# A two-layer fp32 transformer stack on one core: free banks for the first products after each boundary, retention's value products among its gates, and stick-breaking split into weights and values

## The reference, cut to what matters

```python
# first block
h = h + rmsnorm(hybrid_mixer(rmsnorm(h)))            # gated delta rule + convolution module
h = h + rmsnorm(memory_cross_attention(rmsnorm(h)))  # 4 heads of 256
h = h + rmsnorm(conv_glu_ffn(rmsnorm(h)))            # up 2*2816, causal conv, silu(a)*b, down
# second block, layer 0: retention, 4 heads, q and k 256 wide, v and gate 512 wide
q = rope(q); k = rope(k) / 16
o_t = sum_{s<=t} gamma_h^(t-s) (q_t . k_s) v_s
o = (o - mean(o)) * rsqrt(var(o) + eps);  y = (o * silu(g)) @ ret_w_out
# second block, layer 1: stick-breaking attention, 8 heads, q and k 128 wide, v 256 wide
A[t,s] = sigmoid(z_ts) * prod_{s<j<t} (1 - sigmoid(z_tj)),   s < t,   z = q k^T / sqrt(128)
y = ((A @ v) * silu(g)) @ sb_w_out
```

## Time and profile before

| | |
|---|---|
| timed runs, median of 3 | 1875.31 us (1871.51, 1875.31, 1875.56) |
| profiled execution | 1869.74 us, of which the span of instructions is 1868.0 us |
| PE busy | 1778.4 us, 95% of the span, 9647 products |
| PEld, DVE, ACT, POOL busy | 1450.4, 1009.3, 674.2, 177.2 us |
| granted TensorE clock, mean | 0.984 |
| HBM traffic | 144.09 MB read, 78 GB/s over the span |

### The profile page before, as it was taken

The page is one execution under the profiler, slowest core; times in us unless marked ns, Lnnn a source line. Parts: engine busy times, 40 slices in busy tenths (PEclk is TensorE's granted clock), DMA queues, the critical chain, the costliest instruction groups (busy, mean ns, idle before and its releaser), DMA issues.

```text
span 1868.0 us, 23478 instructions
## 1 busy us (share of the span) xinstructions
PE 1778.4 (95%) x9647; PEld 1450.4 (78%) x9647; DVE 1009.3 (54%) x1492; ACT 674.2 (36%) x1002; POOL 177.2 (9%) x155
## 2 busy tenths in 40 slices
PE   6899998999999999999999999999999999999987
PEld 5677787789789888888897776877698777787765
DVE  3668788446426954945864633435455333443434
ACT  4443343445335322322351222222154443434342
POOL 0153544210010000000100000000010000000001
PEclk9999899999999999999999999999999999999999
DMA  5111112242112232322322131322122222222211
GB/s 187 35 47 46 35 59 78 79 147 80 42 61 80 91 105 76 113 90 87 135 74 87 58 103 67 107 73 79 59 80 79 66 70 79 69 89 68 90 46 45
DMA packets 44937, 147.70 MB, mean 79 GB/s; under 512 B 4768, under 2 KB 8736, under 8 KB 44832
## 3 DMA queue, kind: packets, MB, share of 16 engines
q1 hardware_dynamic: 44832, 146.21, 23.7%
HBM read 144.09 MB, written 2.10 MB: 78 GB/s over the span
## 4 chain that ended last, share of the span: by engine, by line
PE 85%; DVE 10%; ACT 2%; issue 2%; POOL 1%; DMA 0%; SPq 0%; DVEq 0%; ACTq 0%; POOLq 0%
PE ps L414 29%; PE ps L409 19%; PE ps L410 18%; PE ps L411 18%; DVE sl L1768 1%; DVE acc L1959 1%; DVE ca L1819 1%; PE ps L1000 1%; DVE y L2137 0%; ACT sh L1148 0%; DMA raw<-in_wqkv 0%; DVE pad L1810 0%; POOL dg L2595 0%; DVE ss L1925 0%; DVE ca L1815 0%
## 5 line engine op out<-in xcount | busy, mean ns | idle before, releaser
L1148 ACT ACTIVATE sh<-raw 128x1024 fp32r<-128x1024 f32 x260 | 271.5, 1054 | 570.1 <-PE ps L411 445.3
L1768 DVE TENSOR_TENSOR sl<-raw,sh 128x1024 fp32r<-128x1024 f32 x260 | 322.6, 1251 | 175.9 <-ACT sh L1148 175.8
L409 PE MATMUL ps<-xh,sh 128*128 128x512 f32 x640 | 264.0, 412 | 3.0 <-DVE up L2265 1.5
L411 PE MATMUL ps<-xl,sh 128*128 128x512 f32 x640 | 252.2, 394 | 0.0
L410 PE MATMUL ps<-xh,sl 128*128 128x512 f32 x640 | 251.8, 393 | 0.0
L409 PE MATMUL ps<-sh,xh 128*128 128x512 f32 x384 | 154.7, 403 | 5.6 <-DVE tm L2350 4.0
L411 PE MATMUL ps<-sl,xh 128*128 128x512 f32 x384 | 149.8, 390 | 0.0
L410 PE MATMUL ps<-sh,xl 128*128 128x512 f32 x384 | 149.7, 390 | 0.0
L409 PEld LDWEIGHTS ps<-xh,sh 128*128 128x128 f32 x640 | 121.8, 190 | 32.6 <-issue 2.8
L410 PEld LDWEIGHTS ps<-xh,sl 128*128 128x128 f32 x640 | 121.9, 190 | 26.0 <-issue 2.6
L411 PEld LDWEIGHTS ps<-xl,sh 128*128 128x128 f32 x640 | 121.5, 190 | 26.4
(11 more groups left out here) (353 smaller groups left out, 3256.5 us busy)
## 6 DMA issues: line engine op xcount, KB each, us to landing
raw<-in_wup SPq DMA_DIRECT2D x44, 512.0 KB, 3.5
raw<-in_wdn SPq DMA_DIRECT2D x24, 512.0 KB, 3.4
raw<-in_rqk SPq DMA_DIRECT2D x16, 512.0 KB, 3.5
raw<-in_rv SPq DMA_DIRECT2D x16, 512.0 KB, 3.5
raw<-in_rg SPq DMA_DIRECT2D x16, 512.0 KB, 4.2
raw<-in_rout SPq DMA_DIRECT2D x16, 512.0 KB, 3.5
raw<-in_sv SPq DMA_DIRECT2D x16, 512.0 KB, 3.4
raw<-in_sg SPq DMA_DIRECT2D x16, 512.0 KB, 3.5
```

The source lines that it names most:

```text
L409: e.matmul(dst, wh, ah, start=start, stop=False, skip_group_check=True)
L411: return e.matmul(dst, wh, al, start=False, stop=stop, skip_group_check=True)
L1148: e.activation(SH[j % NSPL][:], RAW[j % NRAW][:], ACT.Copy).then_inc(*hi(j))
L1768: e.tensor_tensor(SL[j % NSPL][:], RAW[j % NRAW][:], SH[j % NSPL][:].bitcast(F32), ALU.subtract).then_inc(*lo(j))
```

## The change

1. **Free banks** (tables `QB`, `up_bank`, `RVB`, `SVB`): the fifth slab behind a boundary goes to a bank that is free already. In the attention and in the FFN's first part it is bank 6 in place of 0; in retention's first head the value slabs use banks 6, 5, 0, 1 in place of 0, 1, 2, 3; in stick-breaking's first pair 6, 0, 1, 2.
2. **Low parts first**: in the FFN's down products DVE makes the low part of the slab ahead before it adds the finished bank to `y`, and not behind. In the gates of retention it makes it before the background steps. At the end of each part of the up products one low part moves ahead of three convolution taps; a wait of DVE on itself now stands there alone.
3. **Retention**: the value products no longer wait for `gated`, so they stand among the gate slabs; the four products with the gates come after `gated`, all four in one step. `sqb` has four buffers in place of two. One empty step less.
4. **Stick-breaking**: `stick` is cut into `weights` and `values`, and the list is weights(p,0), weights(p,1), values(p,0), values(p,1). `values` waits for the gates and for v. For the last pair the gates come before v (in the weight order too), and ACT copies two of the four v banks. Before the absolute value ACT loads the table set that holds both exp and log, in place of one load before each of these two.
5. **The end**: for the last layer POOL adds only tiles 0 to 3, in both halves; PE adds 4 to 7.

```diff
-        o += [("sv", 4 * p + i) for i in range(4)]
-        o += [("sg", 4 * p + i) for i in range(4)]
+        v, g = [("sv", 4 * p + i) for i in range(4)], [("sg", 4 * p + i) for i in range(4)]
+        o += g + v if p == 3 else v + g
...
+        QB = (0, 1, 2, 3, 6, 1, 2, 3)
+        RVB = ((6, 5, 0, 1), (0, 1, 2, 3), (0, 1, 2, 3), (0, 1, 2, 3))
+        SVB = ((6, 0, 1, 2), (0, 1, 2, 3), (0, 1, 2, 3), (0, 1, 2, 3))
+        def up_bank(part, i):
+            return 6 if part == 0 and i == 4 else i % 4
...
@@ PE, retain @@
-                while not gated[h]:
-                    yield
                 for tb in range(NB):
...
                     rel[B] = [(rtv, ("n", h, tb))]
                     yield
-                yield
+                while not gated[h]:
+                    yield
                 yield
...
@@ PE, stick @@
-            def stick(p, h):
+            def weights(p, h):
...
+            def values(p, h):
+                ZZ = ZZS[h]
                 for et in range(2):
-                    while flow["hold"] or (p, 2 * h + et) not in flow["g"]:
+                    while flow["hold"] or (p, 2 * h + et) not in flow["g"] or p not in flow["v"]:
                         yield
...
-                bg.add(stick(p, 0))
-                bg.add(stick(p, 1))
+                for part in (weights, values):
+                    for h in range(2):
+                        bg.add(part(p, h))
...
+                for part in ("gv" if p == 3 else "vg"):
...
@@ ACT, weights @@
+                e.preload_act_table_set("natural_log_exp_and_others")
...
@@ ACT, v of the last pair @@
+                            for tb in (1, 3):
+                                ac.wait_ge(*used[j + 3 if tb == 3 else (j + 3, tb)])
+                                ac.wait_ge(*stm[("o", p - 1, 1, 1)])
+                                e.activation(VS[:, tb, :], PS[SVB[p][tb]][:], ACT.Copy,
+                                             scale=RC[:, tb:tb + 1]).then_inc(*sta(("v", p, tb)))
...
@@ DVE, up @@
+                if i == 2 * FFN[part][1] - 2 * a0 - 2:
+                    low(j + i + 5)
...
@@ DVE, down products @@
                     if m >= 3:
                         beat(2)
+                    low(j + m + 4)
                     if part:
                         y_add(("y3", part, m), m, j + m, m if m < 3 else m % 4,
                               ya[("y3", m)] if part == 1 else yv[("y3", 1, m)])
-                    low(j + m + 4)
...
@@ DVE, retain @@
-                    if tb >= 2:
-                        ve.wait_ge(*rtv[("g", h, tb - 2)])
-                    e.tensor_scalar(SQB[tb % 2][:], b[:], BN[:, tb, 6:7], BN[:, tb, 8:9], ALU.subtract,
+                    if h:
+                        ve.wait_ge(*rtv[("g", h - 1, tb)])
+                    e.tensor_scalar(SQB[tb][:], b[:], BN[:, tb, 6:7], BN[:, tb, 8:9], ALU.subtract,
                                     ALU.mult).then_inc(*rtv(("n", h, tb)))
+                while not gated[h]:
+                    yield
+                for tb in range(NB):
                     ve.wait_ge(*rta[("g", h, tb)])
                     ve.wait_ge(*rtv[("n", h, tb)])
-                    e.tensor_tensor(GR[:, tb, :], GR[:, tb, :], SQB[tb % 2][:], ALU.mult).then_inc(*rtv(("g", h, tb)))
-                yield
+                    e.tensor_tensor(GR[:, tb, :], GR[:, tb, :], SQB[tb][:], ALU.mult).then_inc(*rtv(("g", h, tb)))
                 yield
...
@@ DVE, gates of retention @@
                 for g in range(4):
+                    low(j + 8 + g + 4)
                     beat(2)
-                    low(j + 8 + g + 4)
...
@@ PE, y_sums; POOL, add_squares @@
+                apart = 4 if hf or b == 5 else 7
-                for k in range(4 if hf else 7, 8):
+                for k in range(apart, 8):
...
-                for k in range(1, 7):
+                for k in range(1, 7 if b < 5 else 4):
```

More of the change, by code:

```diff
@@ L239, in program @@
             BN = alloc(ph, "bn", [128, NB, 10])
-            SQB = [alloc(ph, f"sqb{i}", [128, T]) for i in range(2)]
+            SQB = [alloc(ph, f"sqb{i}", [128, T]) for i in range(4)]
         with ExitStack() as ph:
@@ L1113, in tensor_program @@
                     j += 4
-                tokens(j, X, "b4", (0, 1, 2, 3))
-                for tb in range(NB):
-                    rel[tb] = [(stv, ("v", p, tb))]
-                j += 4
-                for kk in range(4):
-                    slab(j + kk, X2, "2b4", at_bank=[kk])
-                    rel[kk] = [(stv, ("g", p, kk))]
-                    flow["g"].add((p, kk))
-                j += 4
+                for part in ("gv" if p == 3 else "vg"):
+                    if part == "v":
+                        tokens(j, X, "b4", SVB[p])
+                        for tb in range(NB):
+                            rel[SVB[p][tb]] = [(sta, ("v", p, tb)) if p == 3 and tb % 2 else (stv, ("v", p, tb))]
+                        flow["v"].add(p)
+                    else:
+                        for kk in range(4):
+                            slab(j + kk, X2, "2b4", at_bank=[kk])
+                            rel[kk] = [(stv, ("g", p, kk))]
+                            flow["g"].add((p, kk))
+                    j += 4
             while len(bg.todo) > 1:
@@ L1583, in retain @@
                     yield
+                for _ in range(NB):
+                    yield
                 while not gated[h]:
                     yield
-                for _ in range(NB):
-                    yield
-                yield
                 yield
@@ L1650, in scalar_program, with weights @@
                     j += 8
-            flow = {"z": 0, "hold": False, "g": set()}
-            def stick(p, h):
+            flow = {"z": 0, "hold": False, "g": set(), "v": set()}
+            def weights(p, h):
                 ZZ = ZZS[h]
@@ L1733, in scalar_program @@
                     j += 4
[L1734 to L1744 removed]
+                for part in ("gv" if p == 3 else "vg"):
+                    for i in range(4):
+                        beat(2)
+                        ahead(j + i + (4 if p == 3 and part == "v" and i == 3 else 5))
+                        if part == "g":
+                            ac.wait_ge(*stv[("g", p, i)])
+                            e.activation(GS[:, i, :], GS[:, i, :], ACT.Silu).then_inc(*sta(("g", p, i)))
+                            flow["g"].add((p, i))
+                    if part == "v":
+                        if p == 3:
+                            for tb in (1, 3):
[3 more added lines that the diff above has]
+                                             scale=RC[:, tb:tb + 1]).then_inc(*sta(("v", p, tb)))
+                            ahead(j + 8)
+                        flow["v"].add(p)
+                    j += 4
             while len(bg.todo) > 1:
```

93 lines of the change are left out of this document (44 added, 49 removed).

## The result

| | before | changed |
|---|---|---|
| timed runs, median | 1873.56 us (1871.51 to 1875.56, 4 runs) | 1842.68 us (1841.75 to 1843.38, 4 runs) |
| ratio, with its 95% interval | | 0.9835 [0.9818, 0.9852] |
| span of the profiled execution | 1868.0 us | 1841.3 us |

The forecast was 1846 us, with a range from 1836 to 1860. Faster was right. The page after: against the earlier trace rows PE's busy time falls by 5.2 us and its idle time by 21.5, in a span that is 26.7 shorter; the products are nearly the same (six more). The gain is idle time and clock, not work.

The account below looks back on a forecast made before the run. PE was busy for 95% of the span, so its waits were priced. Terms of 8.0 + 1.2 + 11.8 + 7.8 + 0.7 = 29.5 us off the median 1875.31 gave 1845.8, taken as 1846 us, range 1836 to 1860.

Parts of the forecast that it names:

- nine terms: Gains at the changed places: free banks 8.0, low parts 1.2, retention 11.8, stick-breaking 7.8, the end 0.7; sum 29.5 us.
- The remaining wait of the two heads: Retention, heads 1 and 3, before the transposes: a wait of 1.2 us would remain in each after the change.
- The 0.16: Everywhere on PE: a wait costs some 0.16 us more than its number in brackets.
- the banks: Fifth slab behind four boundaries: gains 0.9 attention, 1.7 FFN, 4.3 retention, 1.1 stick-breaking, together 8.0 us.
- Lower clock again in heads 1 and 3: Rival, retention: remaining waits bring the lower clock back, 6 us less gain, 1852 us; chance 0.12.
- Given back: Rival: PE's early start is lost again; free banks give 2, stick-breaking 4, 10 us less, 1856 us; chance 0.13.
- Little gained: Rival: engines wait for each other as before in the last pair, retention gain lost; 8 to 10 us gained; chance 0.07.
- The slower one: Rival, stick-breaking: weights(p,1) in its new place holds PE up at the suffix sums; 1893 us; chance 0.04.
- retention's 11.8: Retention, heads 0 to 3: value products among the gates remove waits and lower clock, gain 11.8 us (7.0 + 6.4 + 0.8 - 2.4).
- The low part ahead of the taps: FFN up products: the low part moved ahead of the taps stands where nothing waits, gain 0.
- The 7.8 of stick-breaking's end: Last gates and output product: wait of 5.2, lower clock of 2.3 and a small wait of 0.3 go, gain 7.8 us.

Follow-up runs that it names:

- the longer chain: Changed kernel with ACT taking the absolute value three times in place of once in each of eight softplus chains, 2.5 us longer each; 1848.72 us, ratio 0.9860.
- 6.35 us more on each chain: Changed kernel with ACT taking the absolute value six times in place of once in each of eight softplus chains; 1881.47 us, ratio 1.0042 to the kernel before.

## Why the prediction was right, and where it was not

**The sum.** All nine terms came within 0.4 of what was measured at their places, 30.0 against 29.5. The way in which each was worked out held: the wait that goes, less the wait that is late next (0.9 and 1.1 in the attention and in stick-breaking, where the scores wait for queries), plus the clock behind the long waits. Undoing banks, retention and stick-breaking one at a time showed each of them by its own wait rows. The remaining wait of the two heads was 1.04 with its 0.16, forecast 1.2. The 0.16 itself is not fixed: by positions the FFN's 1.51 costs 1.83 when the old banks bring it back, and the 1.03 behind the longer chain 1.28. That is part of why the banks gave 0.1 and 0.2 more than forecast in the FFN and in retention.

**The base.** The forecast stood 3.3 above the result: 1.8 because I took the median of three runs, 1875.31, which a fourth put at 1873.56, and 1.4 because the medians differ by 30.9; 0.2 is rounding. The profile of before, at 1869.74, was an uncommonly early one (the lowest of the timed runs beside the experiments has 1870.52), and in a part that is the same in both kernels. One `dg,one` row, ahead of all changed places, stands here in the kernel before, in the changed kernel, and in the kernel before with one load:

```profile
376.97 1.10 PE L414 MATMUL ps<-dg,one 128*128 128x512 f32 x2 [1.70 <-DVE dg L1773]
```

```profile
380.40 1.10 PE L422 MATMUL ps<-dg,one 128*128 128x512 f32 x2 [1.72 <-DVE dg L1798]
```

```profile
381.93 1.10 PE L414 MATMUL ps<-dg,one 128*128 128x512 f32 x2 [1.73 <-DVE dg L1774]
```

Over the 14 profiles this row lies between 376.97 and 383.26, and the code of before alone has 376.97 and 381.93; the -3.4 of the table is this. The last of the three has the code of before and 37.4 us at the lower clock, as the changed kernel. So the change need not be its cause, and nothing in the medians speaks for it: the spans differ by 26.7, the changed places by 30.0, the medians by 30.9.

**Rivals.** Lower clock again in heads 1 and 3: no, 1.00 in the window. Given back: none of the banks' gain; 0.4 in stick-breaking's pairs 1 and 2, which I had at nothing and whose cause is open. Little gained: no. The slower one did not happen, but it had its mechanism right and its place wrong. I had asked when `sp` is late for the suffix sums, with a margin of 3.6 in the gates (3.5 shown). In the output product's slabs the same chain holds up the emptying of a bank, with 1.4 of margin, and I had called that stretch safe because it had no waits before. With 6.35 us more on each chain the kernel falls behind the one before, and so far earlier than that rival had it: its sum asked for a chain of 21.8, 11 us more than the 10.8 counted.

**Costs taken as nothing that were not.** The low parts moved ahead in retention's gates: I found no wait that they end in the order of before (they were not tried there alone), but 3.3 of retention's 11.8 hang on them. I had listed the edit and not asked what covers it in the new order: DVE now waits for PE's value products inside the gates, and what stands behind that wait in its list is late. That retention's term came out at 11.8 all the same is luck: the early low parts were in the change, priced at nothing. The low part ahead of the taps was probably worth 0.4: PE's wait of 0.22 ahead of a down product is gone, and stays gone when the other low parts are late again, but no run undid this edit alone.

**A term with two causes.** The 7.8 of stick-breaking's end I gave to the split alone. 1.34 of the wait belonged to the second table load. But the load alone, put into the kernel before, gained 0.7 by positions and nothing that the medians show, since the stretch of lower clock moved with the wait and fell more on products; with the split undone and the load kept, 5.8 of the 7.6 came back. So the parts do not add up: undone one at a time, banks, retention, stick-breaking and the small edits give 9.7, 13.4, 5.8 and 5.5 us by positions, 34.3 in all before rounding, where together they gave 30.0. The excess is the low parts (3.3, counted in retention's 11.8 too) and more lower clock with old banks and old retention (1.6 each), less 1.8 in stick-breaking and the 0.4 of the taps, which no run undid.

**The skill against the trace.** The Trainium skill ("ScalarE: Activation LUTs", "Rules for kernel authors") has about 2.7 us for a switch of table sets and wants activations grouped by set. The load took 1.28 in every trace here, and nothing stood beside it: in the rows of the eighth chain above it starts 0.02 behind the activation before it, the next starts 0.01 behind it, and a chain with two loads takes 1.27 more than one with a single load (6.45 and 5.18, from its first load or activation to the end of the logarithm). So here the trace does not agree, and 1.28 is the whole price of a switch. At that price a second load in the thinly covered chains cost nothing (1844.82 against 1843.10), since 1.4 was covered; the page's figure would not have fitted under that cover, as the run with 2.5 us more showed with its 3.4. One set for both functions took 1.34 off the last wait of the kernel before and nothing that its medians show off its time.

## What to carry to other kernels

Where one engine is nearly always busy, price an edit by the wait that goes and by the one that is late next, read at that place, and add the lower clock that stands behind long waits; the sum of such terms was right to 0.5 of 30 us here, with 0.4 unforeseen on either side. When a step moves, look at everything queued behind its waits on each engine, for each stretch it can fall into: both misses here (3.3 us in retention that hung on the early low parts, 1.4 of cover in place of 3.6 in stick-breaking) were low parts or bank emptyings behind a wait, in stretches that had shown no wait before. And compare positions of the same instruction in the two traces, since two executions of unchanged code can differ by several us before the change begins.

## What the runs showed of the hardware that was not expected

- The same code ahead of the first changed place ended between 376.97 and 383.26 us over 14 profiles. The granted clock up to 375 is 0.93 to 0.95. PE's start, between 13.13 and 14.83 us, explains little of it: counted from there the row still lies between 363.0 and 368.8, and what the rest hangs on is open.

```profile
0.00:375.00 375.00, 327.51 (x2663) 266.46 (x2663) 249.43 (x349) 149.63 (x222) 126.81 (x98) 0.95 0.21 70
```

```profile
0.00:375.00 375.00, 330.56 (x2641) 269.15 (x2641) 249.72 (x347) 148.30 (x221) 126.27 (x97) 0.93 0.21 70
```

The first row is the kernel before, the second the one with the old order in retention.

- The same waits don't always bring the lower clock. Waits of 1.60 and 2.38 left it at 1.00 in the kernel before and the same at 0.91 with old banks in the changed kernel; the wait of 3.67 had 0.83 in the 20 us around it in the kernel before with one load, and 0.91 in the changed kernel with the old stick-breaking. What decides between them is open; it wasn't tried.
